# Rotary embedding of four retention heads: half-swaps copied by ScalarE, cosine products and sums on GpSimd, row factors spread by TensorE transpositions

## The chip, the core and the metric

The kernel runs on one core of one Trainium2 chip. The metric is the device time of one execution in microseconds (us). The engines are PE (TensorE, with its weight load PEld), DVE (VectorE), ACT (ScalarE), POOL (GpSimd) and SP (SyncE).

## The reference

Two transformer blocks follow one another on x of 512 tokens by 1024 features: a mix of dilated attention and a state-space layer with a feed-forward layer, then a mix of a convolution of width 31 and a retention layer with four heads of 128 features, a gated feed-forward layer and a gated side input. Many RMS norms stand between them. What the change touches is the rotary embedding of the retention heads, and the norms' factors:

```python
def rotary(t, pos):
    half = t.shape[-1] // 2
    ...
    t1, t2 = t[..., :half], t[..., half:]
    return jnp.concatenate([t1 * cos - t2 * sin, t1 * sin + t2 * cos], axis=-1)
...
    q = rotary(hq.reshape(shp).astype(jnp.float32), pos)
    k = rotary(hk.reshape(shp).astype(jnp.float32), pos) * (RET_HEAD_DIM ** -0.5)
...
def rmsnorm_2(x, w):
    y = xf * lax.rsqrt(jnp.mean(xf * xf, axis=-1, keepdims=True) + EPS)
```

## The kernel before

Features lie on the 128 partitions, the 512 tokens along the free axis. All weights come as one stream of slots (here called units) of 128 x 1024 numbers, one unit for one output of 128 features, in a ring of four. For each unit SP loads `raw`, ACT rounds it to `w_hi` (`split`, line 1002), POOL makes `w_lo = raw - w_hi` in two halves of 512 columns (`low_half`, line 368), and PE does 8 x 3 products of 128 x 512 (`exact`, lines 395 to 397), 24 to a unit. ACT splits unit u + 4 when PE has ended unit u (`refill`), so PE finds its weights made three units ahead.

The second block's mix (phase "mix2") has eight units a, b for the convolution, then for each head h = 0 to 3 the units q2, k2, v2, g2, then eight output units out2. All engines run hand-written lists of instructions in order; semaphores join them.

**Per head.** ACT copies q2, k2 and v2 out of PSUM (`head_in`, line 1514) to `r_q`, `r_k`, `r_v`, each followed by the refill of its slot. After unit v2, PE multiplies `r_q` and `r_k` by the permutation `perm` (`swaps`, lines 812 and 814), which puts each head's lower 64 features in the place of the upper and the reverse, in PSUM banks 4 and 5. DVE then does `rotate(h)` (lines 2373 to 2377): for q and for k the product with the cosines `rt[:, 0]`, the product of the swapped half with the signed sines `rt[:, 1]` into `rot_s`, a drain, and the two sums. PE reads the result in `ret_scores(h)` (line 822), which stands after the next head's q2 unit; `decayed(h)` on DVE takes the scores out of PSUM, `ret_values`, a sum of squares (`ret_sum`, line 848), and a norm follow, each in the midst of the next head's units. DVE spends the rest of this stretch on the 120 taps of the convolution (`taps`, line 2366), each a 128 x 512 multiply-add into PSUM bank 2 or 3. ACT seeds those banks (`conv_seed`, line 1503) and takes them out (`conv_out`, line 1507).

**Spreading a factor.** A norm's factor is computed by DVE with tokens on the partitions, 128 at a time, in a column of `tiny`. PE spreads it over a PSUM bank: the stationary operand is the column broadcast to 128 x 128, the moving operand the identity. Four such products (two in the halved tails) make a spread, in `half_spread` (443), `stat_broadcast` (520), `y_spread` (673, once for each of 8 groups of the state-space layer) and `spread` (856, for the four heads' row factors and the layer norm):

```python
                for t in range(QB):
                    last = mm(rb[:, t * P:(t + 1) * P], tiny[:, 40 + t:41 + t].broadcast_to([P, P]), ident,
                              start=True, stop=True)
```

PE's `transpose` is used before too, for `r_v` (line 831) and elsewhere, with the data as stationary operand and the same identity as moving operand.

## Time and profile before

| | |
|---|---|
| time, median of 3 runs | 1810.99 us (1809.95 to 1811.51) |
| time of the profiled execution | 1810.07 us |
| its span, first to last instruction | 1808.0 us |
| busy PE / PEld / DVE / ACT / POOL | 1776.3 / 1465.5 / 840.6 / 758.9 / 767.1 us |
| mean granted TensorE clock | 0.999 |
| chain that ended last | PE 94%, DVE 3%, ACT 1% |
| heads' stretch, 1195 to 1297 us: PE / DVE / ACT / POOL busy | 101.7 / 97.0 / 36.9 / 38.5 us of 102 |

Busy time is the sum of the recorded durations of an engine's instructions. PE's durations overlap, since one product's end is modelled past the next one's start; the distance from start to start is what a product costs in a row of products. "Idle before" is the time in which an engine had nothing to do, with the instruction that ended it. A float32 product of two float32 operands leaves two records for each instruction; a transposition leaves one.

### The profile page before, as it was taken

What the parts mean: (1) busy time and instruction counts of PE and PEld (TensorE: products, weight loads), DVE (VectorE), ACT (ScalarE), POOL (GpSimd) and SP (SyncE); (2) the same over time, 40 slices, a digit from 0 to 9 for tenths busy, and PEclk for the clock granted to TensorE, in tenths of its full rate; (3) what the DMA queues carried; (4) which work ended last, traced back from release to release, by engine and by line L of the source; (5) the groups of instructions that cost most, each with busy time, mean ns of one, the idle gap of its engine ahead of it and who ended that gap; (6) DMA issues with size and microseconds to landing.
All of it is one profiled execution on the core that took longest, in us unless ns stands there. A gap on an engine that the chain in (4) does not pass through costs nothing.

```text
span 1808.0 us, 25058 instructions
## 1 busy us (share of the span) xinstructions
PE 1776.3 (98%) x9058; PEld 1465.5 (81%) x9058; DVE 840.6 (46%) x1577; ACT 758.9 (42%) x1248; POOL 767.1 (42%) x590
## 2 busy tenths in 40 slices
PE   7999999999999999999999999999999999999998
PEld 5777788888888888888888888887788888888877
DVE  5554546677676311273111123899937433320044
ACT  5444554566664322353323233534455322222253
POOL 4322344433333545345444444353233444445543
PEclk9999999999999999999999999999999999999999
DMA  5212233332323223233222322232212232233321
GB/s 198 69 59 85 71 116 106 105 105 94 105 94 129 94 94 104 83 116 113 91 100 93 102 96 82 70 105 70 71 59 81 84 104 93 95 103 105 105 82 47
DMA packets 47803, 170.68 MB, mean 94 GB/s; under 512 B 5312, under 2 KB 7488, under 8 KB 47456
## 3 DMA queue, kind: packets, MB, share of 16 engines
q1 hardware_dynamic: 44352, 156.25, 25.7%
q10 hardware_dynamic: 3360, 13.17, 2.2%
q8 instruction: 63, 1.03, 0.2%
q14 instruction: 28, 0.23, 0.0%
HBM read 167.24 MB, written 2.16 MB: 94 GB/s over the span
## 4 chain that ended last, share of the span: by engine, by line
PE 94%; DVE 3%; ACT 1%; issue 0%; DMA 0%; SPq 0%; DVEq 0%; POOLq 0%; POOL 0%; ACTq 0%
PE bank L395 28%; PE bank L397 28%; PE bank L396 28%; PE bank L574 1%; PE bank L722 1%; PE bank L583 1%; PE bank L596 1%; DVE xs L1880 1%; PE bank L726 1%; PE bank L706 1%; PE bank L507 1%; DVE u_lo L1885 1%; PE bank L822 0%; PE bank L840 0%; PE bank L433 0%; PE bank L697 0%
## 5 line engine op out<-in xcount | busy, mean ns | idle before, releaser
L368 POOL TENSOR_TENSOR w_lo<-raw,w_hi 128x512 fp32r<-128x512 f32 x578 | 760.2, 1337 | 1014.8 <-ACT w_hi L1002 1014.5
L395 PE MATMUL bank<-u_hi,w_hi 128*128 128x512 f32 (+1 forms) x1624 | 625.0, 385 | 6.8 <-DVE u_lo L1885 6.5
L397 PE MATMUL bank<-u_hi,w_lo 128*128 128x512 f32 (+1 forms) x1624 | 612.3, 377 | 0.0
L396 PE MATMUL bank<-u_lo,w_hi 128*128 128x512 f32 (+1 forms) x1624 | 611.6, 377 | 0.0
L1002 ACT ACTIVATE w_hi<-raw 128x1024 fp32r<-128x1024 f32 x289 | 304.0, 1053 | 285.5 <-PE bank L397 285.2
L395 PEld LDWEIGHTS bank<-u_hi,w_hi 128*128 128x128 f32 x1624 | 305.4, 188 | 67.7 <-DVE u_lo L1885 7.7
L397 PEld LDWEIGHTS bank<-u_hi,w_lo 128*128 128x128 f32 x1624 | 305.3, 188 | 57.4
L396 PEld LDWEIGHTS bank<-u_lo,w_hi 128*128 128x128 f32 x1624 | 305.8, 188 | 53.6 <-issue 0.5
L395 PE MATMUL bank<-v_hi,w_hi 128*128 128x512 f32 (+1 forms) x368 | 133.8, 364 | 2.7 <-DVE v_lo L2446 2.7
L396 PE MATMUL bank<-v_lo,w_hi 128*128 128x512 f32 (+1 forms) x368 | 133.0, 362 | 0.0
L397 PE MATMUL bank<-v_hi,w_lo 128*128 128x512 f32 (+1 forms) x368 | 133.0, 362 | 0.0
L2037 DVE SCALAR_TENSOR_TENSOR post<-bank,vec,post 128x511 f32<-128x511 f32 (+2 forms) x96 | 71.8, 748 | 27.5 <-ACT post L1151 22.5
L2366 DVE SCALAR_TENSOR_TENSOR bank<-cat,vec,bank 128x512 f32<-128x512 f32 x120 | 83.4, 749 | 1.7 <-ACT bank L1503 0.8
L395 PEld LDWEIGHTS bank<-v_hi,w_hi 128*128 128x128 f32 x368 | 69.5, 189 | 14.3 <-DVE v_lo L2446 3.8
L2297 DVE TENSOR_TENSOR ffn_acc<-ffn_acc,bank 128x512 f32<-128x512 f32 x29 | 19.9, 688 | 127.3 <-PE bank L397 127.3
L397 PEld LDWEIGHTS bank<-v_hi,w_lo 128*128 128x128 f32 x368 | 69.4, 189 | 10.7
L396 PEld LDWEIGHTS bank<-v_lo,w_hi 128*128 128x128 f32 x368 | 69.5, 189 | 10.6
L2285 DVE SCALAR_TENSOR_TENSOR tmp<-bank,tmp 128x512 f32<-128x512 f32 x32 | 22.1, 691 | 118.2 <-ACT tmp L1430 118.2
L1760 DVE TENSOR_TENSOR diag<-diag,sq 128x512 f32<-128x512 f32 x30 | 27.6, 919 | 106.4 <-ACT sq L1019 105.7
L395 PE MATMUL bank<-h_hi,w_hi 128*128 128x512 f32 x176 | 68.5, 389 | 0.0
L396 PE MATMUL bank<-h_lo,w_hi 128*128 128x512 f32 x176 | 68.5, 389 | 0.0
L397 PE MATMUL bank<-h_hi,w_lo 128*128 128x512 f32 x176 | 68.5, 389 | 0.0
(320 smaller groups left out, 2170.4 us busy)
## 6 DMA issues: line engine op xcount, KB each, us to landing
raw<-weights SPq DMA_DIRECT2D x289, 512.0 KB, 3.2
bc<-acs ACTq DMA_DIRECT2D x16, 512.0 KB, 3.9
xs<-x SPq DMA_DIRECT2D x4, 512.0 KB, 5.5
xs<-x ACTq DMA_DIRECT2D x1, 2048.0 KB, 7.5
rt<-ret_tables ACTq DMA_DIRECT2D x1, 1536.0 KB, 6.3
out<-xs SPq DMA_DIRECT2D x12, 128.0 KB, 1.8
dist<-att_tables SPq DMA_DIRECT2D x1, 512.0 KB, 10.7
p_raw<-p ACTq DMA_DIRECT2D x1, 512.0 KB, 7.2
```

Source lines behind the costliest of these rows:

```text
L368: return nc.gpsimd.tensor_tensor(w_lo[:, slot, w], raw[:, slot, w], w_hi[:, slot, w].bitcast(F32), ALU.subtract)
L395: mm(dst, w_hi[:, slot, w], hi, start=first, stop=False)
L396: mm(dst, w_hi[:, slot, w], lo, start=False, stop=False)
L397: return mm(dst, w_lo[:, slot, w], hi, start=False, stop=last)
L507: mm(ps[bank][:, 0:cols], ones, cst[:, 0:cols], start=True, stop=True)
L574: mm(ps[2 + 2 * (step % 2) + h][:, 0:n], q_t[i % 2][rows, s * P:(s + 1) * P], k_t[i % 2][rows, 0:n], start=True, stop=True).then_inc(sem(" ...
L1002: af(w_hi[:, slot, :], raw[:, slot, :], ACT.Copy).then_inc(hi_done, 1)
L1760: tt(diag[:], diag[:], sq[:, c % 2, :], ALU.add).then_inc(sq_used, 1)
L2037: last = stt(out=post[:, now, back:T], in0=ps[job.bank][:, 0:T - back], scalar=vec[:, tap:tap + 1], in1=post[:, now, back:T], op0=ALU.mult ...
L2285: stt(out=tmp[:, j % 2, :], in0=ps[bank][:], scalar=0.0, in1=tmp[:, j % 2, :], op0=ALU.max, op1=ALU.mult).then_inc(out_free[j % 2], 1)
L2297: tt(ffn_acc[:, j, :], ffn_acc[:, j, :], ps[j % 2][:], ALU.add).then_inc(out_free[j % 2], 1)
L2366: stt(out=ps[2 + c % 2][:], in0=cat31[:, c, t:t + T], scalar=vec[:, at:at + 1], in1=ps[2 + c % 2][:], op0=ALU.mult, op1=ALU.add).then_inc( ...
```

## The change

1. PE's `swaps` are gone. ACT does `swapped(h)` after `head_in("k2", h)`: two copies of 64 partitions each for q and for k, from the other half of `r_q` or `r_k` into PSUM bank 4 or 5.
2. DVE's `rotate(h)` keeps the two products with the sines. The two products with the cosines go to POOL for all heads (`cosine_part`), the two sums to POOL for heads 0 to 2 (`rotated_sum`); for head 3 DVE does the sums (`rotated_last`).
3. POOL's loop over the ring's turns is split in three, so that the units from q2 of head 0 to out2's last are written out singly, with POOL's new work between them.
4. All spreads of factors call `transpose` in place of the product, operands unchanged.

```diff
--- before.py
+++ after.py
@@ -102,6 +102,8 @@
 for _n, _job in enumerate(MIX2_ORDER):
     JOBS[_job] = Job(UNIT0["mix2"] + _n, TILES, MIX2_BANKS[_n], _outs[MIX2_BANKS[_n]])
     _outs[MIX2_BANKS[_n]] += 1
+ROTATED_FROM = JOBS["q2", 0].unit // RING * RING
+ROTATED_END = (JOBS["out2", 7].unit // RING + 1) * RING
 
 
 VEC = {}
@@ -368,15 +370,49 @@
                 return nc.gpsimd.tensor_tensor(w_lo[:, slot, w], raw[:, slot, w], w_hi[:, slot, w].bitcast(F32),
                                                ALU.subtract)
 
-            with pool.Fori(0, SLOTS // RING) as g:
+            def low_halves(u):
+                pool.wait_ge(hi_done, u + 1)
+                low_half(u % RING, 0)
+                low_half(u % RING, 1).then_inc(lo_done, 1)
+
+            def cosine_part(part, h, src, dst):
+
+                job = JOBS[part, h]
+                pool.wait_ge(out_free[job.bank], job.m + 2)
+                if h:
+                    pool.wait_ge(sem("r_scores"), 4 * h)
+                else:
+                    pool.wait_ge(sem("tables_scaled"), 2)
+                nc.gpsimd.tensor_tensor(dst[:], src[:], rt[:, 0, :], ALU.mult).then_inc(sem("cosine_part"), 1)
+
+            def rotated_sum(h):
+
+                for j, dst in enumerate((rot_q, rot_k)):
+                    pool.wait_ge(sem("cosine_part"), 2 * h + j + 1)
+                    pool.wait_ge(sem("sine_part"), 2 * h + j + 1)
+                    nc.gpsimd.tensor_tensor(dst[:], dst[:], rot_s[:, j, :], ALU.add).then_inc(sem("rotated"), 1)
+
+            with pool.Fori(0, ROTATED_FROM // RING) as g:
+                for s in range(RING):
+                    pool.wait_ge(hi_done, g * RING + (s + 1))
+                    low_half(s, 0)
+                    low_half(s, 1).then_inc(lo_done, 1)
+            for u in range(ROTATED_FROM, ROTATED_END):
+                low_halves(u)
+                for h in range(R_HEADS):
+                    if u == JOBS["q2", h].unit + RING:
+                        cosine_part("q2", h, r_q, rot_q)
+                    if u == JOBS["k2", h].unit + RING:
+                        cosine_part("k2", h, r_k, rot_k)
+                    if u == JOBS["v2", h].unit + RING and h < R_HEADS - 1:
+                        rotated_sum(h)
+            with pool.Fori(ROTATED_END // RING, SLOTS // RING) as g:
                 for s in range(RING):
                     pool.wait_ge(hi_done, g * RING + (s + 1))
                     low_half(s, 0)
                     low_half(s, 1).then_inc(lo_done, 1)
             for u in range(SLOTS // RING * RING, SLOTS):
-                pool.wait_ge(hi_done, u + 1)
-                low_half(u % RING, 0)
-                low_half(u % RING, 1).then_inc(lo_done, 1)
+                low_halves(u)
 
             for h in range(2):
                 for c in range(1, C8, 2):
@@ -440,8 +476,7 @@
                 pe.wait_ge(factor_ready, k + h + 1)
                 for t in range(2):
                     at = 40 + 2 * h + t
-                    last = mm(rb_half[h][:, t * P:(t + 1) * P], tiny[:, at:at + 1].broadcast_to([P, P]), ident,
-                              start=True, stop=True)
+                    last = nc.tensor.transpose(rb_half[h][:, t * P:(t + 1) * P], tiny[:, at:at + 1].broadcast_to([P, P]), ident)
                 last.then_inc(rb_ready, 1)
 
             def halved_tail(name, unit0, hi, lo):
...
@@ -804,15 +837,6 @@
                     last = exact(ps[job.bank][:], job.unit % RING, t, u_hi[:, t, :], u_lo[:, t, :], t == 0, t == TILES - 1)
                 last.then_inc(out_ready[job.bank], 1)
 
-            def swaps(h):
-
-                if h:
-                    pe.wait_ge(sem("decayed"), 4 * h)
-                evicted(("q2", h))
-                mm(ps[4][:], perm, r_q[:], start=True, stop=True).then_inc(sem("swapped"), 1)
-                evicted(("k2", h))
-                mm(ps[5][:], perm, r_k[:], start=True, stop=True).then_inc(sem("swapped"), 1)
-
             def ret_scores(h):
 
                 pe.wait_ge(sem("rotated"), 2 * h + 2)
@@ -853,8 +877,7 @@
                 pe.wait_ge(sem("row_factor"), factor + 1)
                 for t in range(QB):
                     at = ROW_AT[factor][2] + t
-                    last = mm(ps[bank][:, t * P:(t + 1) * P], tiny[:, at:at + 1].broadcast_to([P, P]), ident,
-                              start=True, stop=True)
+                    last = nc.tensor.transpose(ps[bank][:, t * P:(t + 1) * P], tiny[:, at:at + 1].broadcast_to([P, P]), ident)
                 return last
 
             def ret_spread(h):
@@ -914,7 +937,6 @@
                 if h:
                     ret_values(h - 1)
                 unit2(("v2", h))
-                swaps(h)
                 if h:
                     ret_sum(h - 1)
                 if h < last_head:
@@ -1514,6 +1536,15 @@
                 af(dst[:], ps[job.bank][:], ACT.Copy).then_inc(out_free[job.bank], 1)
                 refill((part, h))
 
+            def swapped(h):
+
+                if h:
+                    act.wait_ge(sem("decayed"), 4 * h)
+                for j, (part, src) in enumerate((("q2", r_q), ("k2", r_k))):
+                    act.wait_ge(out_free[JOBS[part, h].bank], JOBS[part, h].m + 2)
+                    af(ps[4 + j][0:HEAD, :], src[HEAD:P, :], ACT.Copy)
+                    af(ps[4 + j][HEAD:P, :], src[0:HEAD, :], ACT.Copy).then_inc(sem("swapped"), 1)
+
             def gate_tanh(h):
                 job = JOBS["g2", h]
                 act.wait_ge(out_free[job.bank], job.m + 2)
@@ -1560,6 +1591,7 @@
                 if h:
                     values_by_token(h - 1)
                 head_in("k2", h, r_k)
+                swapped(h)
                 if h == 1:
                     conv_out(0)
                     conv_seed(2)
@@ -2336,7 +2368,7 @@
             def tables_scaled():
                 dve.wait_ge(sem("rt_landed"), 16)
                 for k in range(2):
-                    tt(rt[:, k, :], rt[:, k, :], x_scale[:], ALU.mult)
+                    tt(rt[:, k, :], rt[:, k, :], x_scale[:], ALU.mult).then_inc(sem("tables_scaled"), 1)
                 ts(half[:, 0:4], v("ln_b", 0, 4), 0.5, None, ALU.mult)
 
 
@@ -2368,12 +2400,17 @@
 
             def rotate(h):
 
-                for j, (src, dst) in enumerate(((r_q, rot_q), (r_k, rot_k))):
+                for j in range(2):
                     dve.wait_ge(sem("swapped"), h * 2 + (j + 1))
-                    tt(dst[:], src[:], rt[:, 0, :], ALU.mult)
-                    tt(rot_s[:, j, :], ps[4 + j][:], rt[:, 1, :], ALU.mult)
-                dve.drain()
+                    if h:
+                        dve.wait_ge(sem("rotated"), 2 * h)
+                    tt(rot_s[:, j, :], ps[4 + j][:], rt[:, 1, :], ALU.mult).then_inc(sem("sine_part"), 1)
+
+            def rotated_last():
+
+                dve.wait_ge(sem("sine_part"), 2 * R_HEADS)
                 for j, dst in enumerate((rot_q, rot_k)):
+                    dve.wait_ge(sem("cosine_part"), 2 * (R_HEADS - 1) + j + 1)
                     tt(dst[:], dst[:], rot_s[:, j, :], ALU.add).then_inc(sem("rotated"), 1)
 
             def decayed(h):
@@ -2491,6 +2528,7 @@
             taps(119, len(CONV_TAPS))
             ret_rest(2)
             rotate(3)
+            rotated_last()
             for c in range(4):
                 centre(c)
             ret_gate(3)```

(The two hunks left out change `stat_broadcast` and `y_spread` in the same way as the first of `half_spread`.)

What becomes of each engine's list is shown at three places. On PE, the end of unit v2 of head 0 and the start of g2, before (`r_q` and `r_k` are the heads' inputs, `cst` the constants with the permutation, `bank` a PSUM bank):

```order
L396 MATMUL bank<-u_lo,w_hi 128x512
L397 MATMUL bank<-u_hi,w_lo 128x512
L812 MATMUL bank<-r_q,cst 128x512
L814 MATMUL bank<-r_k,cst 128x512
L395 MATMUL bank<-u_hi,w_hi 128x512
```

Now the two rows in the middle are gone and the unit g2 follows v2 directly. On ACT, head 1 from its q input to its v input, now:

```order
L1536 ACTIVATE r_q<-bank 128x512
L1024 ACTIVATE w_hi<-raw 128x1024
L1557 ACTIVATE r_vtok<-bank 128x512
L1536 ACTIVATE r_k<-bank 128x512
L1024 ACTIVATE w_hi<-raw 128x1024
L1545 ACTIVATE bank<-r_q 64x512
L1546 ACTIVATE bank<-r_q 64x512
L1545 ACTIVATE bank<-r_k 64x512
L1546 ACTIVATE bank<-r_k 64x512
L1529 ACTIVATE cv<-bank,vec 128x512
L1525 ACTIVATE bank<-cat_104,vec 128x512
L1565 ACTIVATE sq<-bank 128x512
```

The four rows of 64 x 512 are new; the convolution's `conv_out(0)` and `conv_seed(2)` and the square of head 0 (L1565) stand behind them. On POOL, from the first unit written out singly to head 1, now:

```order
L370 TENSOR_TENSOR w_lo<-raw,w_hi 128x512 x16
L386 TENSOR_TENSOR rot_q<-r_q,rt 128x512
L370 TENSOR_TENSOR w_lo<-raw,w_hi 128x512 x2
L386 TENSOR_TENSOR rot_k<-r_k,rt 128x512
L370 TENSOR_TENSOR w_lo<-raw,w_hi 128x512 x2
L393 TENSOR_TENSOR rot_q<-rot_q,rot_s 128x512
L393 TENSOR_TENSOR rot_k<-rot_k,rot_s 128x512
L370 TENSOR_TENSOR w_lo<-raw,w_hi 128x512 x4
L386 TENSOR_TENSOR rot_q<-r_q,rt 128x512
```

Before, only the rows of `w_lo` stood there. Each cosine product follows the low halves of the unit four ahead of its own.

## Rows read from the trace of the kernel before

**Rows 1.** The page, chain that ended last, by engine

```profile
PE 94%; DVE 3%; ACT 1%; issue 0%; DMA 0%; SPq 0%; DVEq 0%; POOLq 0%; POOL 0%; ACTq 0%
```

**Rows 2.** Windows: busy us and count of PE, PEld, DVE, ACT, POOL; clock; DMA

```profile
30.00:180.00 150.00, 149.90 (x865) 111.40 (x864) 74.71 (x265) 73.52 (x178) 51.31 (x40) 1.00 0.23 78
...
1195.00:1297.00 102.00, 101.66 (x455) 79.28 (x454) 96.99 (x156) 36.85 (x50) 38.48 (x29) 1.00 0.23 74
```

**Rows 3.** Waits of PE, whole span: us in total, times, longest

```profile
PE bank L395 <- DVE u_lo L1885: 6.5, 6, 1.4
...
PE bank L856 <- DVE tiny L2412: 0.3, 1, 0.3
```

**Rows 4.** Timeline of PE at head 0's swaps: start us, length us, line, operands

```profile
1201.88 0.39 PE L397 MATMUL bank<-u_hi,w_lo 128*128 128x512 f32 x1
1202.11 1.02 PE L812 MATMUL bank<-r_q,cst 128*128 128x512 f32 x2
...
1204.05 0.40 PE L396 MATMUL bank<-u_lo,w_hi 128*128 128x512 f32 x1
```

**Rows 5.** Timeline of PE, a spread by four products (row factor, head 0)

```profile
1239.89 1.05 PE L856 MATMUL bank<-cst,tiny 128*128 128x128 f32 x8
...
1241.02 0.39 PE L396 MATMUL bank<-u_lo,w_hi 128*128 128x512 f32 x1
```

**Rows 6.** Timeline of PE, four transpositions of r_v (head 0)

```profile
1216.91 0.60 PE L831 MATMUL bank<-cst,r_v 128*128 128x128 f32 x4
...
1217.58 0.39 PE L396 MATMUL bank<-u_lo,w_hi 128*128 128x512 f32 x1
```

**Rows 7.** Tile tiny on PE: records, ns min/median/max, first and last start

```profile
L673 PE MATMUL bank<-cst,tiny x64: 271/275/275, 277.6 to 585.4; 128*128 128x128 f32 x64
L856 PE MATMUL bank<-cst,tiny x40: 271/275/376, 1239.9 to 1321.2; 128*128 128x128 f32 x40
L520 PE MATMUL bank<-cst,tiny x32: 270/275/519, 15.8 to 1739.1; 128*128 128x128 f32 x32
L443 PE MATMUL bank<-cst,tiny x32: 270/275/376, 771.9 to 1800.1; 128*128 128x128 f32 x32
```

**Rows 8.** Timeline of PE, a spread of two products in the last tail

```profile
1791.20 0.60 PE L443 MATMUL bank<-cst,tiny 128*128 128x128 f32 x4
...
1791.76 0.28 PE L396 MATMUL bank<-u_lo,w_hi 128*128 128x256 f32 x1
```

**Rows 9.** Timeline of DVE, heads 1 to 3

```profile
1233.24 0.85 DVE L2373 TENSOR_TENSOR rot_q<-r_q,rt 128x512 f32<-128x512 f32 x1
1234.02 0.68 DVE L2374 TENSOR_TENSOR rot_s<-bank,rt 128x512 f32<-128x512 f32 x1
...
1237.68 0.17 DVE L2406 RECIPROCAL tiny<-tiny 128x4 f32<-128x4 f32 x1
...
1240.98 0.69 DVE L2421 SCALAR_TENSOR_TENSOR r_g<-r_g,bank 128x512 f32<-128x512 f32 x1 [1.14 <-PE bank L856]
...
1271.13 0.69 DVE L2421 SCALAR_TENSOR_TENSOR r_g<-r_g,bank 128x512 f32<-128x512 f32 x1
...
1295.71 0.16 DVE L2412 SCALAR_TENSOR_TENSOR tiny<-tiny 128x4 f32<-128x4 f32 x1
```

**Rows 10.** Timeline of PE, the spreads for heads 1 and 2

```profile
1270.04 1.05 PE L856 MATMUL bank<-cst,tiny 128*128 128x128 f32 x8
...
1295.93 1.16 PE L856 MATMUL bank<-cst,tiny 128*128 128x128 f32 x8 [0.34 <-DVE tiny L2412]
```

**Rows 11.** Timeline of ACT, head 1: the seed of convolution chunk 2

```profile
1225.25 0.69 ACT L1503 ACTIVATE bank<-cat,vec 128x512 f32<-128x512 f32 x1
```

**Rows 12.** Timeline of POOL, head 1: low halves of one unit

```profile
1232.28 2.97 POOL L368 TENSOR_TENSOR w_lo<-raw,w_hi 128x512 fp32r<-128x512 f32 x2 [5.09 <-ACT w_hi L1002]
```

**Rows 13.** Timeline of PE: scores of head 1; the stage's longest wait

```profile
1244.90 2.32 PE L822 MATMUL bank<-rot_q,rot_k 128*128 128x512 f32 x8
...
1323.64 0.50 PE L395 MATMUL bank<-v_hi,w_hi 128*128 128x512 f32 x1 [2.15 <-DVE v_lo L2446]
```

More of the change, by code:

```diff
@@ L519, in stat_broadcast @@
                 for t in range(QB):
-                    last = mm(rb[:, t * P:(t + 1) * P], tiny[:, 40 + t:41 + t].broadcast_to([P, P]), ident,
-                              start=True, stop=True)
+                    last = nc.tensor.transpose(rb[:, t * P:(t + 1) * P], tiny[:, 40 + t:41 + t].broadcast_to([P, P]), ident)
                 last.then_inc(rb_ready, 1)
@@ L672, in y_spread @@
                 for t in range(QB):
-                    last = mm(ps[6][:, t * P:(t + 1) * P], tiny[:, 40 + t:41 + t].broadcast_to([P, P]), ident,
-                              start=True, stop=True)
+                    last = nc.tensor.transpose(ps[6][:, t * P:(t + 1) * P], tiny[:, 40 + t:41 + t].broadcast_to([P, P]), ident)
                 last.then_inc(sem("ssm_rb"), 1)
@@ L855, in spread @@
                     at = ROW_AT[factor][2] + t
-                    last = mm(ps[bank][:, t * P:(t + 1) * P], tiny[:, at:at + 1].broadcast_to([P, P]), ident,
-                              start=True, stop=True)
+                    last = nc.tensor.transpose(ps[bank][:, t * P:(t + 1) * P], tiny[:, at:at + 1].broadcast_to([P, P]), ident)
                 return last
```

## The prediction

> **What bounds the kernel now.** I read the chain of waits first: PE carries 94% of it [rows 1]. The windows say the same of the place of the change: in the heads' stretch, 1195 to 1297 us, PE is busy all the time, but DVE is busy 97 of 102 us as well, ACT 37 and POOL 38 [rows 2]. So whatever PE no longer does there is gained only as long as DVE, which is nearly full too, comes along. PE's waits are few: six, together 6.5 us, on DVE at the halved norms, and 0.3 us on a row factor in the heads' stretch [rows 3], besides one of 2.15 us before the second mix's last output units [rows 13].
>
> **PE's part, the swaps.** A product of 512 columns costs 0.23 us from start to start (1201.88 to 1202.11). From L812's start to the start of L396, the second product after the swaps, it is 1.94 us; one step would have been there anyway, so the two swaps cost 1.94 - 0.23 = 1.71 us [rows 4]. Four heads: 6.84 us off PE.
>
> **PE's part, the spreads.** From L856 to the L396 behind it 1.13 us, less one step of 0.23: four float32 products cost 0.90 us [rows 5]. The same measure for four transpositions of 128 x 128 in the same stretch, with the identity as moving operand: 0.67 - 0.23 = 0.44 us [rows 6]. Here the stationary operand is a broadcast column and not a tile; I take 0.44, since all else is alike. That saves 0.46 us for four and 0.23 for two. The records of `tiny` (two for each product) make 84 products, so 21 fours: 8 in the state-space layer (L673), 5 in the heads' stage (L856), 4 in whole norms (L520), 16 products in halved norms (L443) [rows 7]. Two products cost 0.56 less a half-width step of 0.12, so 0.44 us, half of a four [rows 8]. All together 21 x 0.46 = 9.7 us at most.
>
> The Trainium skill, in "TensorE: Matmul & The Clock Gate", section "Terms", says that the transpose mode is four times faster for FP32. An estimate by that page would have a spread of 0.90 us fall to 0.23 and the time to about 1792; the trace has two records against one and 0.44 us [rows 5, 6], and the sum goes by these.
>
> Which of them lie on the path:
> - State-space layer: PE does not wait there, all count, 8 x 0.46 = 3.7 us.
> - Whole norms before, in and after the feed-forward layers: three sit between PE's products, 1.4 us. The very first norm has records of up to 519 ns, twice the usual 275 [rows 7]; DVE has nothing to do until it ends, so I count it double, 0.9 us (0.5 as the low bound).
> - Halved norms: eight spreads of 0.23. The first half's lies on the way to DVE's work, for which PE then waits (the six waits of [rows 3]). The second half's falls where DVE is busy with the first half, and is lost in the next of those waits. So four of eight, 0.9 us; bounds 0 and 1.8.
>
> Outside the heads' stage that is 3.7 + 1.4 + 0.9 + 0.9 = 6.9 us.
>
> **The heads' stage.** What DVE loses: `rotate(h)` with its two cosine products and two sums takes 1237.68 - 1233.24 = 4.44 us for head 1; two sine products at 0.68 remain, about 1.3 [rows 9]. DVE gains some 3 us for each head, so it has room for the shorter PE. But it has to come back to PE at each head's norm: before, it waits 1.14 us for head 0's spread (L2421 at 1240.98) [rows 9]. PE comes to head 1's spread earlier by three swaps and one spread, 5.13 + 0.46 = 5.6 us. From there to head 2's spread DVE does a row of norms, taps and scores without any rotation in it: L2421 at 1271.13 to the end of L2412 at 1295.87 is 24.74 us, and the next spread starts 0.06 later [rows 9, 10]. PE needs 1295.93 - 1270.04 = 25.89 us for the same piece, less its wait of 0.34, less the fourth swap 1.71 and the spread 0.46: 23.4 us [rows 10]. DVE needs 25.4: 24.74, 0.06, and 0.63 from the spread's start to DVE (1.09 in [rows 5, 9], less 0.46). So **the fourth swap buys almost nothing before that point**: PE will stand about 2.0 us before head 2's spread, and is ahead of its old time by 5.6 + 0.46 = 6.05 us there. Behind it come three spreads (head 2's, the layer norm's, head 3's) with everything waiting for them: + 1.4. The stage gives 7.4 us; the wait of 2.15 us [rows 13] moves along, since its chain starts at those spreads.
>
> **What is added, and what hides it.** ACT gets four copies a head of 64 x 512. The nearest row is an ACT write of SBUF data to PSUM, 0.69 us for 128 x 512 [rows 11]; half the partitions may cost the same, so 2.4 to 2.8 us a head and at least 1.4. ACT is idle two thirds of the stretch. Queued behind them at head 1 is the seed of convolution chunk 2 (L1503), for which DVE's taps wait: DVE will stand there up to 3 us or so, which eats what it won by the lighter rotation of head 0, and PE's next need of DVE (head 0's spread at 1239.89) has DVE's 1.14 us of waiting and 3 us of head 1's rotation as cover. Nothing on the path, if copies are not much dearer. POOL gets 14 operations of 128 x 512. Its own halves take 2.97 us for two at worst [rows 12], so 1.3 to 1.5 us each, 18 to 21 us on 38 busy of 102 [rows 2]. The sums come last: for head 1 after the low halves that end at 1235.25, so at about 1238 by the old time; PE reads them at 1244.90 [rows 13], and comes some 3.9 us earlier. Cover 3 us. If that is gone, PE waits at each scores product. Low halves are late by the same 3 us, against a unit of 24 x 0.23 = 5.5 us and a lead of three units. The last head's sums stay on DVE, whose rotation there falls from 4 to 2.6 us; the loop's split costs POOL some branches: nothing.
>
> **Sum.** 6.9 + 7.4 = 14.3 us. The profiled execution took 1810.07 us, 2.07 more than its span, and lies 0.9 under the median of 1810.99; the same gain from it would be 1795.8, from the median 1796.7. I forecast **1796.7 us**.
>
> **The rivals.**
> 1. *ACT or POOL set the heads' pace.* Copies that cost twice the 0.69 us put 5.5 us before the seed at head 1, or sums on POOL come 3 us too late. Then the swaps' gain before head 1's spread is lost, about 5 us: 1802. Against it: ACT's 37 us and POOL's 38 of 102. Chance 0.09.
> 2. *The transpositions do not do what they say*, because a broadcast column loads as slowly as before: 0.90 stays. Then swaps alone: 5.1 us at head 1's spread, and from there DVE's 25.9 us leave nothing more: 1805.9. Chance 0.04.
> 3. *They cost less still*, 0.23 for four: about 4 us more of gain, 1792. Against it [rows 6]. Chance 0.03.
> 4. *PE's clock falls, the side of slower.* After each spread of transpositions PE could be granted 1.2 GHz for the products that follow. Were it one unit each time, 24 products at 0.46 in place of 0.23, 21 times 5.5 us would be lost and the time 1912. It decides from 14.3 / 21 = 0.68 us a spread on, three products at the half clock. Against it: between 30 and 180 us, where the attention's transpositions run among the units, the clock is 1.00 [rows 2]. Chance 0.02.
>
> The Trainium skill speaks for this fourth case: "TensorE: Matmul & The Clock Gate", section "Part 4: PE-mode transpose", says that transpose-mode work does not count as PE-busy for the clock's monitor. The row at 1.00 disagrees as far as it can, four to a burst among dense products.
>
> The forecast's own case, with its bounds, has 0.82.
>
> **How the numbers follow.** The best bound is all 9.7 us of spreads, 0.5 for the first norm and 6.8 of swaps, 17.0: 1794.0, less a run's scatter. The other side takes in the first rival's milder half. Range 1793.3 to 1801.0. The cases below 1807.4 (faster by 0.2%, about what a measurement of this kernel can tell from no change) are all but the fourth and some of the second: faster 0.95, same 0.03, slower 0.02.
>
> **What would show it.** The spreads' records halve in number (84 in place of 168) and take 0.44 us to the next unit; the windows of the state-space layer shorten by 3.7 us. From the heads' first unit to the stage's end 7.4 us are gone. PE's wait for L2412's successor rises from 0.34 to about 2 us. ACT's new copies take 0.6 to 0.7 us, POOL's new work 1.3 to 1.5. I am wrong if the scores wait for POOL, if PE's wait at head 2's spread is over 4 us or absent, or if a transposition of the broadcast column costs 0.2 us and more.

## The result, and the profile after

| | before | changed |
|---|---|---|
| median, us | 1811.07 (1809.95 to 1811.51) | 1799.39 (1798.22 to 1799.60) |
| ratio of the times | | 0.9936 (0.9921 to 0.9950) |
| profiled execution, us | 1810.07 | 1799.22 |
| its span, us | 1808.0 | 1797.4 |

The kernel is 11.7 us faster by the medians and 10.85 us by the two profiled executions; 14.3 us were forecast. The time lies inside the range, 2.7 us above the forecast of 1796.7.

The page of the changed kernel, the busy times and the chain that ended last:

```profile
PE 1762.0 (98%) x8958; PEld 1453.6 (81%) x8958; DVE 834.5 (46%) x1563; ACT 768.0 (43%) x1264; POOL 783.5 (44%) x604
...
PE 90%; DVE 7%; ACT 1%; issue 1%; DMA 0%; DVEq 0%; SPq 0%; POOLq 0%; POOL 0%; ACTq 0%
```

PE is still the bound, but DVE's part of the chain went from 3% [rows 1] to 7%: in the heads' stage the chain now runs through DVE, from 1223.8 to 1286.7 us. The records of `tiny` on PE in the changed kernel (records, ns min/median/max, first and last start), to be set beside [rows 7]:

```profile
L707 PE MATMUL bank<-cst,tiny x32: 271/273/273, 277.5 to 581.6; 128*128 128x128 f32 x32
L880 PE MATMUL bank<-cst,tiny x20: 271/272/322, 1233.5 to 1311.0; 128*128 128x128 f32 x20
L555 PE MATMUL bank<-cst,tiny x16: 271/272/476, 15.8 to 1727.9; 128*128 128x128 f32 x16
L479 PE MATMUL bank<-cst,tiny x16: 270/298/421, 768.1 to 1789.6; 128*128 128x128 f32 x16
```

There are 84 records in place of 168, each about as long as before: a spread is halved, no more. Head 0's stands below: 1233.53 to 1233.88 is 0.35 us to the next product, which itself takes 0.32 to the one behind it, so 0.67 in all, less a step of 0.23 that is 0.44, the figure of [rows 6]. PE's waits in the changed kernel (us in total, times, longest), beside [rows 3]:

```profile
PE bank L431 <- DVE u_lo L1917: 8.2, 6, 1.7
PE bank L431 <- DVE v_lo L2483: 2.7, 3, 2.1
PE bank L880 <- DVE tiny L2449: 1.9, 1, 1.9
```

Timeline of PE in the changed kernel: head 0's scores, the spreads for heads 0, 1 and 2, the stage's last long wait (start us, length us, line, operands, the wait ahead of it):

```profile
1210.13 0.59 PE L846 MATMUL bank<-rot_q,rot_k 128*128 128x512 f32 x1
...
1233.53 0.60 PE L880 MATMUL bank<-cst,tiny 128*128 128x128 f32 x4
1233.88 0.48 PE L431 MATMUL bank<-u_hi,w_hi 128*128 128x512 f32 x1
1234.20 0.39 PE L432 MATMUL bank<-u_lo,w_hi 128*128 128x512 f32 x1
...
1261.48 0.60 PE L880 MATMUL bank<-cst,tiny 128*128 128x128 f32 x4
...
1286.74 0.65 PE L880 MATMUL bank<-cst,tiny 128*128 128x128 f32 x4 [1.90 <-DVE tiny L2449]
...
1313.44 0.50 PE L431 MATMUL bank<-v_hi,w_hi 128*128 128x512 f32 x1 [2.14 <-DVE v_lo L2483]
```

The wait before head 2's spread is 1.90 us, against 0.34 before the change [rows 10] and 2.0 forecast; the wait of 2.15 [rows 13] has moved along at 2.14. No product waited for ACT's copies or for POOL's cosines and sums. Those took (ACT's copies of 64 x 512; POOL's cosine products for q; its sums took 1.29 us too, as shown at e10):

```profile
L1545 ACT ACTIVATE bank<-r_q x4: 593/593/597, 1195.6 to 1275.9; 64x512 f32<-64x512 f32 x4
L1546 ACT ACTIVATE bank<-r_q x4: 598/599/601, 1196.2 to 1276.5; 64x512 f32<-64x512 f32 x4
...
L386 POOL TENSOR_TENSOR rot_q<-r_q,rt x4: 1282/1290/1302, 1192.9 to 1272.6; 128x512 f32<-128x512 f32 x4
```

DVE did wait once. Its taps of convolution chunk 2 need the seed, which stands on ACT behind head 1's four copies:

```profile
1223.83 5.36 DVE L2398 SCALAR_TENSOR_TENSOR bank<-cat,vec,bank 128x512 f32<-128x512 f32 x8 [2.60 <-ACT bank L1525]
```

From there to the end of PE's wait at 1286.74 DVE has no other wait, so the chain that ended last runs over ACT's copies and the seed to DVE and to that spread.

**Where the time went, place by place.** The same product of the two kernels, its start before less its start after, is what has been gained up to there:

| up to | before, us | after, us | gained so far | this piece |
|---|---|---|---|---|
| first units (the very first norm) | 20.18 | 20.02 | 0.16 | 0.16 |
| end of the state-space layer | 767.69 | 763.94 | 3.75 | 3.6 |
| first product after a wait | 1147.81 | 1144.06 | 3.75 | 0 |
| first whole unit after it | 1156.75 | 1154.33 | 2.42 | -1.3 |
| head 0's scores | 1214.75 | 1210.13 | 4.62 | 2.2 |
| end of the heads' stage | 1328.92 | 1318.72 | 10.20 | 5.6 |
| late in the feed-forward part | 1738.31 | 1727.53 | 10.78 | 0.6 |
| the norm behind it | 1746.32 | 1735.08 | 11.24 | 0.5 |
| last tail, keep_clock | 1794.51 | 1783.06 | 11.45 | 0.2 |
| last tail, last spread | 1799.68 | 1789.35 | 10.33 | -1.1 |
| span | 1808.0 | 1797.4 | 10.6 | 0.3 |

Two pieces are negative, and no term of the sum was. The first begins at one of PE's longer waits. Timeline of PE in the changed kernel there, and the windows around it (busy us and count of PE, PEld, DVE, ACT, POOL; granted clock; DMA):

```profile
1144.06 0.39 PE L431 MATMUL bank<-u_hi,w_hi 128*128 128x256 f32 x1 [1.68 <-DVE u_lo L1917]
...
1145.76 0.41 PE L431 MATMUL bank<-u_hi,w_hi 128*128 128x256 f32 x1
1145.97 0.41 PE L432 MATMUL bank<-u_lo,w_hi 128*128 128x256 f32 x1
```

```profile
1144.00:1146.00 2.00, 1.94 (x14) 1.94 (x15) 2.00 (x7) 1.14 (x3) 0.00 (x0) 0.87 0.45 156
1146.00:1148.00 2.00, 2.00 (x11) 2.00 (x11) 2.00 (x6) 1.91 (x4) 0.00 (x0) 0.50 0.27 107
```

Half-width products that step by 0.12 us step by 0.21 us after 1145.5: the granted clock is 0.50, 1.2 GHz in place of 2.4, after PE stood 1.68 us and worked on for over a microsecond. In the last tail the clock falls at 1787.2, where the keep_clock products (idle products of ones, in the kernel before as well) run at half speed; there PE's only wait shortly before is one of 0.59 us, and what it did from 1785.1 to 1786.9 was products of one column. The profiled execution before had no such stretch before 1804, behind its last spread, so the comparison of the two profiles charges 1.3 us to the change and, at the end, 0.9 (11.45 less 10.6).

**An execution has a second thing that varies, at the very first norm.** The last small operation of DVE's factor starts there within 0.25 us of the start of a low half on POOL. In the changed kernel's profile above it starts at 15.56, just ahead of POOL's 15.57, and takes 0.16 us. When the same kernel was profiled again (r, below), it started at 15.70, behind POOL's 15.64:

```profile
15.70 1.23 DVE L1812 SCALAR_TENSOR_TENSOR tiny<-tiny 128x4 f32<-128x4 f32 x1
```

PE then waited 0.99 us for the factor, and the first units started 1.1 us later than in the kernel before, in place of 0.16 us sooner. Of the fourteen profiles of this case five show the late form (r, e2, e4, e5, e10), all others, that of the kernel before too, the early one. It moves a time by some 1.2 us and has nothing to do with the clock, so a difference of about 1 us between medians of five executions shows little, below.

### The profile page after: what moved, and what is told of

Read it like the earlier page. It is cut to its first block, busy times and chain, and to the rows that moved or that the text cites. A ratio compares the mean times of both kernels' runs of the same rounds, so it can differ in the third digit from the quotient of the medians.

```text
span 1797.4 us, 24798 instructions
## 1 busy us (share of the span) xinstructions
PE 1762.0 (98%) x8958; PEld 1453.6 (81%) x8958; DVE 834.5 (46%) x1563; ACT 768.0 (43%) x1264; POOL 783.5 (44%) x604
## 3 DMA queue, kind: packets, MB, share of 16 engines
q8 instruction: 62, 1.02, 0.2%
## 4 chain that ended last, share of the span: by engine, by line
PE 90%; DVE 7%; ACT 1%; issue 1%; DMA 0%; DVEq 0%; SPq 0%; POOLq 0%; POOL 0%; ACTq 0%
PE bank L431 28%; PE bank L433 27%; PE bank L432 27%; DVE bank L2398 2%; PE bank L608 1%; PE bank L755 1%; PE bank L617 1%; PE bank L630 1%; DVE xs L1912 1%; PE bank L759 1%; DVE u_lo L1917 1%; PE bank L739 1%; PE bank L542 1%; PE bank L469 0%; PE bank L730 0%
## 5 line engine op out<-in xcount | busy, mean ns | idle before, releaser
L370 POOL TENSOR_TENSOR w_lo<-raw,w_hi 128x512 fp32r<-128x512 f32 x578 | 759.1, 1336 | 987.1 <-ACT w_hi L1024 987.0
L431 PE MATMUL bank<-u_hi,w_hi 128*128 128x512 f32 (+1 forms) x1624 | 625.0, 385 | 8.7 <-DVE u_lo L1917 8.2
L432 PE MATMUL bank<-u_lo,w_hi 128*128 128x512 f32 (+1 forms) x1624 | 612.2, 377 | 0.0
L1024 ACT ACTIVATE w_hi<-raw 128x1024 fp32r<-128x1024 f32 x289 | 303.9, 1053 | 280.8 <-PE bank L433 280.3
L431 PEld LDWEIGHTS bank<-u_hi,w_hi 128*128 128x128 f32 x1624 | 306.2, 189 | 69.8 <-DVE u_lo L1917 9.4
L432 PEld LDWEIGHTS bank<-u_lo,w_hi 128*128 128x128 f32 x1624 | 306.5, 189 | 53.3 <-issue 0.2
L431 PE MATMUL bank<-v_hi,w_hi 128*128 128x512 f32 (+1 forms) x368 | 133.9, 364 | 2.7 <-DVE v_lo L2483 2.7
L432 PE MATMUL bank<-v_lo,w_hi 128*128 128x512 f32 (+1 forms) x368 | 133.0, 361 | 0.0
L2398 DVE SCALAR_TENSOR_TENSOR bank<-cat,vec,bank 128x512 f32<-128x512 f32 x120 | 83.5, 750 | 4.3 <-ACT bank L1525 3.4
L431 PEld LDWEIGHTS bank<-v_hi,w_hi 128*128 128x128 f32 x368 | 69.4, 189 | 14.5 <-DVE v_lo L2483 3.8
L432 PEld LDWEIGHTS bank<-v_lo,w_hi 128*128 128x128 f32 x368 | 69.5, 189 | 10.5
L431 PE MATMUL bank<-h_hi,w_hi 128*128 128x512 f32 x176 | 68.5, 389 | 0.0
L432 PE MATMUL bank<-h_lo,w_hi 128*128 128x512 f32 x176 | 68.5, 389 | 0.0
```

The costliest lines, as they stand in the source:

```text
L370: return nc.gpsimd.tensor_tensor(w_lo[:, slot, w], raw[:, slot, w], w_hi[:, slot, w].bitcast(F32), ALU.subtract)
L431: mm(dst, w_hi[:, slot, w], hi, start=first, stop=False)
L432: mm(dst, w_hi[:, slot, w], lo, start=False, stop=False)
L1024: af(w_hi[:, slot, :], raw[:, slot, :], ACT.Copy).then_inc(hi_done, 1)
L2398: stt(out=ps[2 + c % 2][:], in0=cat31[:, c, t:t + T], scalar=vec[:, at:at + 1], in1=ps[2 + c % 2][:], op0=ALU.mult, op1=ALU.add).then_inc( ...
```

## The experiments

**The two halves of the change apart.** The changed kernel's four spreads written back as products, all else kept (e2); and the kernel before with the spreads alone transposed (e1):

```diff
# e2, against the changed kernel; the same in all four spreads
-    last = nc.tensor.transpose(ps[bank][:, t * P:(t + 1) * P], tiny[:, at:at + 1].broadcast_to([P, P]), ident)
+    last = mm(ps[bank][:, t * P:(t + 1) * P], tiny[:, at:at + 1].broadcast_to([P, P]), ident, start=True, stop=True)
# e1, against the kernel before: the reverse edit
```

> The kernel before with nothing but the transposed spreads. The changed kernel's trace gives 3.6 us in the state-space layer, 0.2 at the first norm, nothing for the halved norms' first three tails, 0.5 for each whole spread behind; with the five spreads of the heads' stage that is about 7.5 us: 1803.6 us. The theory that PE's clock falls because transpositions stand near DVE's waits (or because these waits are longer by 0.3 us) expects one or two stretches of half clock, mean clock 0.998 or less and up to 2 us more: 1804 to 1805.7. The rival, that the falls come only from where a wait happens to lie in time, expects them here in some runs or none.

Measured: 1804.14 us (1803.91 to 1804.57) against 1810.88 before, ratio 0.9964 (0.9950 to 0.9977): 6.7 us. Its five executions had a mean clock of 0.996 to 0.998; the profile has one inner stretch of half clock, at 1319.5, behind PE's wait of 2.15 us.

> The changed kernel with all spreads as products again: swaps on ACT, cosines and sums on POOL. PE is ahead by three swaps, 5.1 us, at head 1's spread; from there to head 2's DVE needs all of 25.9 us, so the fourth swap gives nothing: 5.1 to 5.4 us, 1805.8 us, with PE waiting about 1.7 us for head 2's row factor. If POOL or ACT were in the way it would be above 1807. Both theories of the clock (transpositions, or longer waits behind them) expect no half clock before the end: mean clock 0.999.

Measured: 1805.25 us (1804.32 to 1805.94), ratio 0.9968 (0.9956 to 0.9980): 5.6 us. That the swaps with POOL's share alone give 5.6 and not the 6.84 that they take off PE bears out "the fourth swap buys almost nothing": PE waits 1.9 us before head 2's spread in e2 as well. The two parts add up to 12.4 us, 0.7 more than the 11.7 of the whole. In e2's profile the clock falls at 1320.6, behind the wait of 2.15 us, and its executions split into three with a mean clock of 0.999 and three with 0.996 to 0.997, where I had expected 0.999 throughout. So the stretches at half clock need no transposition.

**The halved norms.** Only their spreads as products again (e3), or each transposed twice (e7):

```diff
# e3, in half_spread
-    last = nc.tensor.transpose(rb_half[h][:, t * P:(t + 1) * P], tiny[:, at:at + 1].broadcast_to([P, P]), ident)
+    last = mm(rb_half[h][:, t * P:(t + 1) * P], tiny[:, at:at + 1].broadcast_to([P, P]), ident, start=True, stop=True)
# e7, in half_spread
-    for t in range(2):
+    for t in (0, 1, 0, 1):
```

> The changed kernel with the halved norms' spreads as products. Their transposition won nothing in the three inner tails and 0.2 us in the last. If the two stretches of half clock come from the transpositions or from the longer wait behind them, they go away, the mean clock is 0.999, and the time falls by 1.3 + 0.9 us to about 1797.3. If they come from the place in time alone, one or both may stay, and the time is 1798 to 1799.4.

> The changed kernel with each halved norm's spread transposed twice, so four transpositions take the 0.44 us that two products took: PE's waits for DVE are as long as before the change, but all of PE's work there is transposition. If the clock falls because the waits are longer, it does not fall here: clock 0.999, 1797.3 us. If it falls because transpositions do not count as work, it still falls: 0.997, 1799.4 us.

Measured: e3 1798.60 us (1798.23 to 1799.86), ratio 0.9935 (0.9922 to 0.9949); e7 1799.48 us (1798.15 to 1800.64), ratio 0.9937 (0.9924 to 0.9951). Each was expected at 1797.3 us if its edit took the half clock away; neither did (mean clocks 0.995 to 0.998 in both). The halved transposition wins nothing that can be measured; PE's six waits go back from 8.2 us to 6.5 in e3 and 6.8 in e7, so what PE saves there it waits. The rows say why. Timelines of DVE and of POOL at one halved norm in the changed kernel:

```profile
1352.20 0.87 DVE L1906 SCALAR_TENSOR_TENSOR y_u<-y_u,vec,bank 128x256 f32<-128x256 f32 x2 [0.64 <-PE bank L479]
1352.99 1.11 DVE L1912 TENSOR_TENSOR xs<-xs,y_u 128x256 f32<-128x256 f32 x1
...
1354.42 1.11 DVE L1912 TENSOR_TENSOR xs<-xs,y_u 128x256 f32<-128x256 f32 x1
```

```profile
1352.54 2.72 POOL L370 TENSOR_TENSOR w_lo<-raw,w_hi 128x512 fp32r<-128x512 f32 x2 [1.22 <-ACT w_hi L1024]
```

And in the kernel before, where all stands 10.2 us later:

```profile
1363.04 0.87 DVE L1874 SCALAR_TENSOR_TENSOR y_u<-y_u,vec,bank 128x256 f32<-128x256 f32 x2 [1.26 <-PE bank L443]
1363.83 0.48 DVE L1880 TENSOR_TENSOR xs<-xs,y_u 128x256 f32<-128x256 f32 x1
...
1364.62 1.12 DVE L1880 TENSOR_TENSOR xs<-xs,y_u 128x256 f32<-128x256 f32 x1
```

```profile
1362.73 2.73 POOL L368 TENSOR_TENSOR w_lo<-raw,w_hi 128x512 fp32r<-128x512 f32 x2 [1.20 <-ACT w_hi L1002]
```

DVE starts 0.64 us sooner (1363.04 less 10.2 is 1352.84), but its add of two SBUF tiles, 0.48 us when it starts as POOL's first low half ends, takes 1.11 when it starts early under it, and ends where it would have ended anyway: 1354.10 against 1364.31 less 10.2. The operations with a PSUM operand beside it (L1906) keep their 0.47. The Trainium skill, "GPSIMD Engine Reference", section "1. Specifications", says that GpSimd shares its SBUF interfaces with VectorE and that VectorE's instructions with two SBUF inputs contend for them. By that rule, which these rows bear out, L1912 stretches and L1906 does not; what it costs is in the rows.

**POOL's share of the rotation.** ACT's copies and the transposed spreads kept, cosines and sums all on DVE as before the change (e4):

```diff
# e4, against the changed kernel; DVE
-    tt(rot_s[:, j, :], ps[4 + j][:], rt[:, 1, :], ALU.mult).then_inc(sem("sine_part"), 1)
...
+    tt(dst[:], src[:], rt[:, 0, :], ALU.mult)
+    tt(rot_s[:, j, :], ps[4 + j][:], rt[:, 1, :], ALU.mult)
# and without cosine_part and rotated_sum on POOL
```

> The changed kernel with the whole rotation on DVE again; only the swaps are moved, to ACT, and the spreads are transposed. If DVE's room is what let PE's gain through, as the prediction has it, the stage gives about 3 us less: DVE was idle for only 2.9 us of the heads' stretch before, 1802.4 us. If PE alone sets the pace there, POOL's share buys nothing and the time stays at 1799.4 us.

Measured: 1808.67 us (1806.79 to 1809.04), ratio 0.9980 (0.9971 to 0.9989): 3.1 us under the kernel before in place of 11.7. POOL's share, which saves PE nothing, is worth some 8 us by the ratios. And e4 has all that e1 has and the swaps off PE besides, yet e1 was at 0.9964: on its own, taking 6.84 us of swaps off PE gained nothing, and by the medians it cost some 3 us (the two intervals just overlap). PE's waits in e4, and the window of the heads' stretch (as in [rows 2]):

```profile
PE bank L844 <- DVE tiny L2408: 7.8, 3, 2.9
```

```profile
1195.00:1297.00 102.00, 94.21 (x418) 74.87 (x418) 99.81 (x154) 45.38 (x65) 37.79 (x28) 0.98 0.23 75
```

DVE, busy 99.8 of 102 us, is the bound there now, and PE 94.2. PE waits at three heads' spreads instead of one, 5.9 us more than in the changed kernel and 6.9 more than in e1 (0.5 at a spread, 0.4 at the scores), as much as the swaps take off it. The clock falls to half at 1237.5 and at 1295.5, just behind waits of 2.87 and 2.30 us, so a part of the 8 us is the clock's (mean 0.994 to 0.997). And at head 0 the factor's small operations lie under POOL's low halves (1233.63 to 1236.37), 2.1 us in place of 0.3:

```profile
1234.20 0.97 DVE L2404 SCALAR_TENSOR_TENSOR tiny<-tiny 128x4 f32<-128x4 f32 x1
1235.25 1.15 DVE L2406 TENSOR_TENSOR tiny<-tiny 128x4 f32<-128x4 f32 x1
```

My expectation had counted the waits too low, and the clock and this not at all.

**Which part of POOL's share.** Cosines on POOL, all sums on DVE (e10):

```diff
# e10, against the changed kernel
-    rotated_sum(h)                 # POOL, heads 0 to 2
...
+    dve.wait_ge(sem("sine_part"), 2 * h + 2)
+    dve.wait_ge(sem("cosine_part"), 2 * h + j + 1)
     # the two sums, at every head in rotate(h)
```

> The changed kernel with the cosine products on POOL and all sums on DVE. DVE has 1.3 us more ahead of the factors of heads 0 and 1, where PE comes 0.6 us after the factor now: PE waits 0.7 us at each, so 1 to 1.5 us above the changed kernel. The all-or-nothing rival (POOL's operations themselves slow DVE, and fewer of them is as good) says no slower than the changed kernel.

Measured: 1798.64 us (1797.71 to 1800.08), ratio 0.9929 (0.9915 to 0.9943), beside the changed kernel's 1799.66 on the same chip. No slower, against the expectation. The row factor of head 0 on DVE in the changed kernel, behind head 1's sine products, and head 1's sums on POOL beside it:

```profile
1229.17 1.28 DVE L2407 TENSOR_TENSOR rot_s<-bank,rt 128x512 f32<-128x512 f32 x2
1230.37 0.17 DVE L2443 RECIPROCAL tiny<-tiny 128x4 f32<-128x4 f32 x1
1230.62 0.84 DVE L2445 SCALAR_TENSOR_TENSOR tiny<-tiny 128x4 f32<-128x4 f32 x1
1231.53 1.17 DVE L2447 TENSOR_TENSOR tiny<-tiny 128x4 f32<-128x4 f32 x1
1232.79 0.16 DVE L2449 SCALAR_TENSOR_TENSOR tiny<-tiny 128x4 f32<-128x4 f32 x1
```

```profile
1230.15 1.29 POOL L393 TENSOR_TENSOR rot_q<-rot_q,rot_s 128x512 f32<-128x512 f32 x1
1231.40 1.29 POOL L393 TENSOR_TENSOR rot_k<-rot_k,rot_s 128x512 f32<-128x512 f32 x1
```

And the same piece of DVE in e10:

```profile
1229.04 1.28 DVE L2398 TENSOR_TENSOR rot_s<-bank,rt 128x512 f32<-128x512 f32 x2
1230.36 0.69 DVE L2403 TENSOR_TENSOR rot_q<-rot_q,rot_s 128x512 f32<-128x512 f32 x1
...
1231.82 0.16 DVE L2434 SCALAR_TENSOR_TENSOR tiny<-tiny 128x4 f32<-128x4 f32 x1
...
1232.30 0.16 DVE L2438 SCALAR_TENSOR_TENSOR tiny<-tiny 128x4 f32<-128x4 f32 x1
```

Operations on 128 x 4 numbers with two SBUF inputs take 0.84 and 1.17 us while POOL adds, each until POOL's operation ends, and 0.16 when it does not. The two sums that DVE takes over cost it 1.2 us and give back 1.7; from the sine products' start the factor is ready after 3.42 us (1229.04 to 1232.46) in place of 3.78 (1229.17 to 1232.95). So of POOL's share the cosines carry the gain, and the sums none. Whether e10 is faster than the changed kernel, by the 1.0 us of the medians, can't be told: its profile has no fall of the clock inside the stage, and that of the changed kernel beside it has two. (Both have the late form of the first norm.)

**What holds the fourth swap back.** The stage's wait of 1.90 us stands for it. Three ways to take it away. The row factor for head 2 two taps earlier (e5):

```diff
# e5, in DVE's program
-    taps(done + 7, done + 27 if h == 0 else 115)
+    taps(done + 7, done + 27 if h == 0 else 113)
...
     ret_var(2)
-    taps(115, 117)
+    taps(113, 115)
     row_factor(ROW["ret", 2])
```

> The changed kernel with DVE's variance, factor and norm of head 2 two taps earlier. If PE's wait of 1.9 us is the lost fourth swap, it falls to 0.4 us; then the rotation of head 3 on DVE, which ends 0.7 us before PE wants it now, is late next, so 0.7 us are won: 1798.7 us. If the wait is no loss, nothing changes: 1799.4 us.

Measured: 1798.76 us (1798.15 to 1800.29), ratio 0.9926 (0.9912 to 0.9939), and the wait still 1.78. The row of DVE in e5 names what is late next:

```profile
1285.32 0.18 DVE L2443 RECIPROCAL tiny<-tiny 128x4 f32<-128x4 f32 x1 [0.79 <-ACT tiny L1570]
1285.58 0.70 DVE L2445 SCALAR_TENSOR_TENSOR tiny<-tiny 128x4 f32<-128x4 f32 x1
```

DVE now waits for ACT's root (L1570), and the operation behind it runs under POOL. PE then waits 0.65 us for head 3's rotation, as expected. That e5 gained anything is not shown: by its profile the stage gave 6.8 us against the changed kernel's 7.3, without a fall of the clock in it. The last head's sums on POOL as well, its sine products ahead of the factor (e6):

```diff
# e6
-    if u == JOBS["v2", h].unit + RING and h < R_HEADS - 1:   # POOL
+    if u == JOBS["v2", h].unit + RING:
...
-    taps(115, 117)                                            # DVE
+    rotate(3)
     row_factor(ROW["ret", 2])
```

> As the one before, and head 3's sine products stand right behind head 2's variance, its sums go to POOL as well. Then the rotation is no longer late; the last taps are, by some 0.6 us. 1.2 us won: 1798.2 us. The rival, that POOL's sums come late there too: 1799.4 us or above.

Measured: 1803.08 us (1801.31 to 1803.24), ratio 0.9950 (0.9936 to 0.9963); worse. The wait became 3.74 us, and by the profile the stage gave 4.0 us in place of 7.3, a fall of the clock at 1286.9 included. DVE in e6:

```profile
1283.84 0.71 DVE L2445 SCALAR_TENSOR_TENSOR tiny<-tiny 128x4 f32<-128x4 f32 x1
1284.62 1.14 DVE L2447 TENSOR_TENSOR tiny<-tiny 128x4 f32<-128x4 f32 x1
1285.84 1.14 DVE L2449 SCALAR_TENSOR_TENSOR tiny<-tiny 128x4 f32<-128x4 f32 x1
```

POOL's four operations from 1282.02 to 1286.96 lie over all three, which take 3.0 us in place of 0.5. Last, on top of the filled waits below, the spread itself later in PE's order and the sums on POOL where they meet no factor (e9):

```diff
# e9, PE; DVE has rotate(3) right behind row_factor(ROW["ret", 2])
-    unit2(("g2", last_head), {3: lambda: ret_spread(last_head - 1), 5: lambda: conv_mean(0, 3)})
+    unit2(("g2", last_head), {5: lambda: conv_mean(0, 3), 7: lambda: ret_spread(last_head - 1)})
```

> The filled waits, and PE's spread for head 2 four tiles later in unit g2, where DVE's factor has long come, and head 3's sine products right after that factor with the sums on POOL, so that POOL does not work during DVE's factor. PE's wait of 1.9 us goes; the last taps are late next by about 0.8 us: 1.1 us below the run before this one. The rival, that DVE's total of taps and norms sets the end of the stage in any order, says within 0.3 us of it.

Measured: 1799.94 us (1798.37 to 1801.08), ratio 0.9939 (0.9926 to 0.9953), 1.6 us over e8b on the same chip. PE's waits in e9:

```profile
PE bank L893 <- ACT cv L1533: 3.0, 1, 3.0
```

The wait at the spread is gone and stands, larger, before the convolution's mean: DVE, now 2.06 us idle for the late spread, is late there. My expectation (1.1 us below e8b) and its rival (within 0.3) both missed. Asking later gains nothing, since DVE has work behind that spread that PE needs in turn.

One thing was not tried. DVE's only wait between 1214 and 1286 us is the 2.60 us for the seed behind ACT's copies. The seed alone ahead of the copies should bring little: DVE reaches head 1's norm at 1262.12, 0.64 us after PE's spread for it starts (1261.48), and the prediction had 0.63 from a spread's start to DVE, so by this estimate PE lets it start no sooner. But with some taps moved from behind that norm to ahead of it, DVE could use the 2.60 us and be sooner at head 2's factor.

**The clock.** Idle products put into PE's waits, which leave every output as it was: two or three of 256 columns at the halved norms, two keep_clock products before the fourth of the eight chunks of the second mix's output products, one more in the last tail (e8, and again as e8b beside the changed kernel, r):

```diff
# e8, e8b
+    if c == 0:
+        for _ in range(2 + h):
+            mm(ps[banks[0]][:, HALF[h]], ones, cst[:, 0:H], start=True, stop=True)
     pe.wait_ge(u_ready, ready0 + h * TILES + c + 1)
...
     ret_spread(last_head)
+    keep_clock(2)
...
-    keep_clock(2, bank=0, cols=3 * P)
+    keep_clock(3, bank=0, cols=3 * P)
```

> The changed kernel with PE doing idle products of ones in its waits for DVE: two or three of 256 columns at each halved norm's waits, two of 512 at the wait of 2.1 us before the second mix's output units, one more of 384 before the last sums. They fit into the waits by the trace. If the stretches of half clock come from these waits, they are gone in all runs: clock 0.999, 1797.2 us and hardly any scatter. If they do not depend on the waits, half of the runs still show 0.996 to 0.998 and the median is 1799 us or so.

> The changed kernel as it is, on the same chip as the next three, so that differences of half a microsecond can be read: 11.7 us under the kernel before, ratio 0.9936.

> The filled waits once more beside the changed kernel. If the half-clock stretches come from the waits, its median is 1 us or more below the changed kernel's here (the clock's share at two places, 1.3 and 0.9 us, in the runs that have them) and none of its runs shows less than 0.998. If the fillers do nothing, both medians agree within 0.5 us.

Measured: e8 1798.53 us (1797.24 to 1799.79), ratio 0.9926 (0.9912 to 0.9939); e8b 1798.34 us (1797.52 to 1799.04), ratio 0.9928 (0.9915 to 0.9942); the changed kernel beside e8b 1799.66 us (1799.48 to 1800.57), ratio 0.9936 (0.9922 to 0.9949). PE's waits in e8b:

```profile
PE bank L431 <- DVE u_lo L1921: 1.7, 6, 0.4
```

In the profiles of e8 and e8b the clock falls only in the last tail (1789.6 and 1792.5); in that of the changed kernel run again it falls at 1287.4 and at 1314.7, behind the wait of 1.91 us and at the end of that of 2.15, and at 1789.1. The unfilled profiles of e5, e7 and e10 have no inner fall either, so single profiles prove little; seven of ten unfilled ones have it, none of the three filled (e9 is the third). The mean clocks say the same: 0.997 to 0.999 in the 15 filled executions, 0.995 to 0.998 in the nine of the changed kernel. That the fillers raise the clock is likely and not certain: e5, unfilled, had 0.997 to 0.999 as well.

What that is worth in time is less clear. e8b is 1.3 us below the changed kernel by the medians, and none of its executions was as slow as the fastest of that kernel, but the intervals of the two ratios overlap, and the changed kernel's profile has the late first norm (1.1 us) and e8b's has not. "Hardly any scatter" was wrong: e8's executions at one mean clock of 0.998 lie between 1797.24 and 1799.79 us, so the clock is not all that varies. One of e8b's five still had 0.997, against my "none". e8b has the lowest median that was measured; e3, e5, e8 and e10 lie within 0.5 us of it.

## Why the prediction was right, and which of its steps failed

- **Bound and mechanism: right.** The heads' stage, from the first swap to its end, gave 7.3 us (10.20 less 2.42 and less 0.46 of a norm) against 7.4 forecast, by the way forecast: PE was 5.7 us ahead at head 1's spread (5.6 forecast; 1270.04 less 1261.48, less the 2.88 gained before the stage), 6.3 at head 2's (6.05), the fourth swap lost in a wait of 1.90 us (2.0), and 1.0 came behind it (1.4). The state-space layer gave 3.6 against 3.7, the whole norms about 1.5 against 1.4. A transposition costs 0.44 for four as taken, which leaves nothing of rivals 2 and 3.
- **The added work: right.** Copies of 0.60 us (0.6 to 0.7 forecast), POOL's new operations 1.29 (1.3 to 1.5), DVE's wait for the seed 2.60 (up to 3). PE waited for none of it directly, so rival 1 did not come. What I gave no weight is that POOL's operations lengthen DVE's small ones, by 1.7 us at head 0's factor. "DVE has room for the shorter PE" held because POOL took the cosines: e4 shows how it goes without.
- **The step that failed first: "the very first norm ... I count it double, 0.9 us".** The spread went from 1.81 us to 0.91 as counted (15.84 to 17.65, now 15.78 to 16.69), and of it 0.16 arrived. DVE before and after at its first unit:

```profile
17.90 1.41 DVE L1801 SCALAR_TENSOR_TENSOR sq<-xs,vec,bank 128x512 f32<-128x512 f32 x2 [2.17 <-PE bank L520]
19.34 0.69 DVE L1795 TENSOR_TENSOR u_lo<-sq,u_hi 128x512 fp32r<-128x512 f32 x1
```

```profile
16.94 1.41 DVE L1833 SCALAR_TENSOR_TENSOR sq<-xs,vec,bank 128x512 f32<-128x512 f32 x2 [1.21 <-PE bank L555]
18.38 1.49 DVE L1827 TENSOR_TENSOR u_lo<-sq,u_hi 128x512 fp32r<-128x512 f32 x1
```

  DVE starts 0.96 us sooner, and its subtraction then runs under POOL's low halves (15.57 to 21.02) for 1.49 us in place of 0.69. DVE had "nothing to do until it ends", but it did not have the SBUF to itself afterwards. That is 0.7 of the missing 2.7 us.
- **"So four of eight, 0.9 us" at the halved norms: 0.2.** The same mechanism, told at e3. It is 0.7 again, and lay within its bounds of 0 and 1.8.
- **Rival 4, the clock: the mechanism named was not there, another was.** It does not follow transpositions: e2, without one, and e3, without those of the halved norms, show the falls too, and where the Trainium skill's sentence on the transpose mode ("TensorE: Matmul & The Clock Gate", "Part 4: PE-mode transpose") would have them, at the 32 transpositions of the state-space layer, the piece gave its full 3.6 us. The inner stretches of half clock came behind waits of 1.7 to 2.9 us in the profiles of the changed kernel and of e1 to e4, and the executions with filled waits had on the whole a higher clock. That the waits are the cause is likely and not shown: others as long have no fall behind them (2.14 us before 1313.44 in the changed kernel's profile, with the clock at 1.00), and the last tail has one with no wait over 0.59 us. The kernel before pays too, by its mean clocks: of its ten executions beside e1 to e7 five had a mean clock of 0.999 and took 1809.99 to 1810.79 us, five 0.996 and took 1810.96 to 1812.75. The profiled one, 1810.07, was of the first kind, which I set aside as a matter of 0.9 us to the median. The changed kernel's four had 0.996 to 0.998. So it seems to pay this price a little more often. That is the rest: 0.7, 0.7 and, by the profiles, 2.2 for two stretches, against small gains of 0.1 to 0.2 elsewhere, make the 3.45 us between 14.3 and 10.85; by the medians, where before paid as well, 2.6 us are missing. What share of those the late form of the first norm has, no run shows; the two profiles compared both have the early one.

**What stays open.** What decides, in one execution and not in the next, whether a wait of 1.7 us is followed by the half clock. How often the late first norm comes in either kernel, since only the profiled executions show it. Whether e3, e5, e7, e8b or e10 differ from the changed kernel at all: the clock and the first norm move each execution by 1 to 2 us. The filled waits and the sums on DVE together (e8b with e10), and the earlier seed with moved taps, were not tried.

## What to carry to other kernels

When PE is the bound and gets less to do, ask of each engine that feeds it how soon it can follow; here DVE was full beside it, and taking 6.84 us of swaps off PE gained nothing (e4) until a part of DVE's work went to POOL, which was worth 8 us or so. Work that is pulled forward on DVE may land under a POOL operation: an operation with two SBUF inputs then ended no sooner than POOL's (0.16 us became up to 1.23), so look at what POOL does in the new place, and not only at DVE's old duration. And judge a gain of under 2 us by several executions with the granted clock beside each, and by the gain up to the same instruction in the profiles: one stretch at half clock cost 1.3 us here, and one small operation at the start 1.2.
